# A two-block transformer kernel on one core: Fourier mixing folded along tokens, layer-norm tiles added before their sum over features, eight low halves formed by an accumulating DMA, rotary partners by shuffle

## The reference

```
def _fourier_mix(v, fw):
    vg = v.reshape(b, l, B_GROUPS, B_GROUP_DIM)            # 256 tokens, 4 groups of 128
    f = jnp.fft.fftn(vg, axes=(1, 3), norm='ortho').real
    return jnp.einsum('blgd,gde->blge', f, fw).reshape(b, l, B_WIDTH)

def _even_mix(h, ...):
    a_val, a_glu, a_gate, b_val, b_gate = _split(h @ w_in, ...)
    u = a_val * jax.nn.sigmoid(a_glu)
    u = jax.nn.silu(_layernorm(_dwconv(u, a_conv_w) + a_conv_b, a_ln_g, a_ln_b))
    y_a = (u @ a_pw_w + a_pw_b) * jax.nn.silu(a_gate)
    y_b = _fourier_mix(b_val, b_fw) * jax.nn.silu(b_gate)
    return jnp.concatenate([y_a, y_b], axis=-1) @ w_out
```

## Time and profile before

| | |
|---|---|
| median of 3 runs | 758.84 us (757.06 to 758.9) |
| the profiled execution | 758.82 us, of which the span is 756.7 us |
| PE busy / DVE busy / ACT busy | 98% / 86% / 51% of the span |
| POOL busy | 1.3 us, 10 instructions |
| granted TensorE clock, mean | 0.999 |
| HBM traffic | 154 MB read, 205 GB/s over the span |

### The profile page before, as it was taken

The page is one execution under the profiler, slowest core; times in us unless marked ns, Lnnn a source line. Parts: engine busy times, 40 slices in busy tenths (PEclk is TensorE's granted clock), DMA queues, the critical chain, the costliest instruction groups (busy, mean ns, idle before and its releaser), DMA issues.

```text
span 756.7 us, 12710 instructions
## 1 busy us (share of the span) xinstructions
PE 739.7 (98%) x5242; PEld 675.0 (89%) x5244; DVE 648.1 (86%) x1062; ACT 383.3 (51%) x530; POOL 1.3 (0%) x10
## 2 busy tenths in 40 slices
PE   8899999999999999999999999999999999999996
PEld 3689979999989999999999988888778899999995
DVE  5877799897998999999888999999989977788653
ACT  4264365668366554544566542222464345555642
POOL 0000000000000000000000000000000000000000
PEclk9999999999999999999999999999999999999999
DMA  9989999866555666666745252121106542575101
GB/s 365 418 320 402 376 386 348 317 246 239 176 215 213 234 223 244 256 231 252 252 159 174 101 225 99 70 98 69 56 0 247 215 141 91 177 278 215 56 2 55
DMA packets 23723, 155.92 MB, mean 206 GB/s; under 512 B 2630, under 2 KB 4463, under 8 KB 5232
## 3 DMA queue, kind: packets, MB, share of 16 engines
q1 hardware_dynamic: 21404, 150.37, 53.3%
q10 hardware_dynamic: 2262, 4.75, 2.0%
HBM read 154.04 MB, written 1.07 MB: 205 GB/s over the span
## 4 chain that ended last, share of the span: by engine, by line
PE 85%; DMA 6%; DVE 6%; ACT 2%; issue 1%; DVEq 0%; ACTq 0%; SPq 0%
PE psum L1529 70%; DMA raw<-in_w 4%; PE psum L1620 2%; DVE w_lo L896 2%; DMA arena<-in_w 2%; DVE w_lo L929 2%; ACT w_hi L400 1%; PE psum L1861 1%; PE psum L2034 1%; PE psum L2058 1%; PE psum L2046 1%; PE psum L1847 1%; PE psum L1711 1%; PE psum L1568 1%; PE psum L1693 1%
## 5 line engine op out<-in xcount | busy, mean ns | idle before, releaser
L1529 PE MATMUL psum<-h_hi,w_hi 128*128 128x256 f32 (+1 forms) x1280 | 386.9, 302 | 2.4 <-DVE w_lo L929 1.2
L1529 PE MATMUL psum<-h_lo,w_hi 128*128 128x256 f32 (+1 forms) x1280 | 382.5, 299 | 0.0
L1529 PE MATMUL psum<-h_hi,w_lo 128*128 128x256 f32 (+1 forms) x1280 | 382.5, 299 | 0.0
L1529 PEld LDWEIGHTS psum<-h_hi,w_hi 128*128 128x128 f32 x1280 | 244.5, 191 | 13.8 <-issue 2.6
L1529 PEld LDWEIGHTS psum<-h_lo,w_hi 128*128 128x128 f32 x1280 | 244.7, 191 | 8.0 <-issue 0.5
L1529 PEld LDWEIGHTS psum<-h_hi,w_lo 128*128 128x128 f32 x1280 | 244.6, 191 | 7.6
L929 DVE TENSOR_TENSOR w_lo<-raw,w_hi 128x2048 fp32r<-128x2048 f32 x90 | 205.9, 2288 | 28.7 <-ACT w_hi L400 27.7
L400 ACT CAST w_hi<-raw 128x2048 fp32r<-128x2048 f32 x90 | 171.2, 1905 | 38.5 <-DMA raw<-in_w 29.5
L896 DVE SCALAR_TENSOR_TENSOR w_lo<-raw,cond 128x1024 fp32r<-128x1024 f32 x88 | 104.2, 1220 | 0.8
L896 DVE SCALAR_TENSOR_TENSOR w_lo<-raw,arena 128x1024 fp32r<-128x1024 f32 x48 | 56.8, 1220 | 11.6 <-ACT arena L450 6.6
L621 ACT ACTIVATE arena<-psum,vec 128x256 f32<-128x256 f32 x44 | 22.5, 564 | 58.6 <-DVE g_lo L1171 54.2
(11 more groups left out here) (239 smaller groups left out, 707.4 us busy)
## 6 DMA issues: line engine op xcount, KB each, us to landing
raw<-in_w SPq DMA_DIRECT2D x138, 1024.0 KB, 5.0
arena<-in_w SPq DMA_DIRECT2D x3, 1024.0 KB, 13.9
xs<-in_xs SPq DMA_DIRECT2D x1, 1024.0 KB, 9.5
consts<-diff ACTq DMA_DIRECT2D x4, 256.0 KB, 10.1
cond<-diff ACTq DMA_DIRECT2D x1, 1024.0 KB, 8.7
xs<-in_xs ACTq DMA_DIRECT2D x1, 1024.0 KB, 7.4
out<-xs SPq DMA_DIRECT2D x2, 384.0 KB, 2.5
consts<-in_c ACTq DMA_DIRECT2D x1, 512.0 KB, 3.9
```

Of the source, the lines that this page charges most:

```text
L1529: last = mm(out, w[a], x[b], start=start and n == 0, stop=stop and n == 2, skip_group_check=skip)
```

## The change

1. Eight low halves (chunks `LIN_EIN`+4 to +11, `BY_DMA`): DVE no longer subtracts. ACT, after the cast, writes -`w_hi` into `w_lo` (a copy with scale -1), and a DMA issued by POOL adds `raw` onto it in SBUF, one such DMA at a time. Waits for `lo_done` become `remainder_ready`, which for these chunks waits for the DMA.
2. Fourier mixing: POOL folds the token axis about its middle (even and odd parts, three 128x508 operations for each pair of groups). The transform along features then makes 128 columns per matmul in place of 256, and that along tokens contracts over 128 in place of 256. The middle token comes in as a column (`fourier_middle`, four matmuls of 2 columns) that DVE adds when it gates. Groups 0 and 1 and the middle are moved ahead of PE's last projection chunk. ACT no longer copies the result out of PSUM; DVE gates straight from it, in four operations of 128x128 for each group in place of one of 128x512.
3. Layer norm: DVE adds the four tiles (and later their squares), so PE makes one sum by ones in place of four, twice.
4. `final_scaled`: four of eight tiles move behind the second `LIN_EOUT` chunk on DVE.
5. Rotary: partners by `stream_shuffle` on DVE in place of the swap matmuls; half of the queries' work moves ahead of `norm("odd_ctx", 7)`.
6. The constant tables get smaller (0.25 MB less to load).

The diff, cut to its core: removed lines stand in the functions printed above and are repeated only where the order of calls changes.

```diff
+BY_DMA = tuple(range(LIN_EIN + 4, LIN_EIN + 12))
+def remainder_of(j):
+    if j in BY_DMA:
+        return "lo_added", 16 * (BY_DMA.index(j) + 1)
+    return "lo_done", j + 1 - AS_LOADED - sum(i < j for i in BY_DMA)
...
+            def fold_tokens(pair):
+                pool.wait_ge(sem("ein_evac"), pair + 5)
+                v = b_val[:, 2 * pair:2 * pair + 2, :].rearrange("p g (s n) -> p (g s) n", s=2)
+                low, high = v[:, :, 1:P], v[:, :, P + 1:T][:, :, ::-1]
+                nc.gpsimd.tensor_tensor(high, low, high, ALU.subtract).then_inc(sem("differences"), 1)
+                pool.wait_ge(sem("differences"), 2 * pair + 1)
+                nc.gpsimd.tensor_tensor(low, low, low, ALU.add).then_inc(sem("differences"), 1)
+                pool.wait_ge(sem("differences"), 2 * pair + 2)
+                nc.gpsimd.tensor_tensor(low, low, high, ALU.subtract).then_inc(sem("folded"), 1)
+            for n, j in enumerate(BY_DMA):
+                if n in (3, 4):
+                    fold_tokens(n - 3)
+                pool.wait_ge(sem("negated"), n + 1)
+                if n:
+                    pool.wait_ge(sem("lo_added"), 16 * n)
+                pool.dma_start(w_lo[:, j % SPL, :].bitcast(F32), raw[:, RAW_OF_LIN[j] % RAW, :],
+                               accum_op=ALU.add).then_inc(sem("lo_added"), 16)
...
+                if i == 9:
+                    act.wait_ge(sem("fold_done"), 2)
+                    nc.scalar.activation(middle[:, 0:8], bank[1][:, 0:8], ACT.Copy, scale=DFT_SCALE).then_inc(sem("fold_ready"), 1)
+                    nc.scalar.activation(middle[:, 8:16], bank[1][:, 0:8], ACT.Copy, scale=-DFT_SCALE).then_inc(sem("fold_ready"), 1)
+                    fourier_evac(0)
+                    fourier_evac(1)
...
-            for g in range(2):
-                fourier_evac(g + 1)
-                fourier_out(g)
...
-            fourier_evac(3)
...
+                if t < 2:
+                    fourier_evac(t + 2)
+            act.wait_ge(sem("ln_sum"), 2)
+            me.mark(nc.scalar.activation(rstd[:, :], bank[3][:, :], ACT.Ln, bias=EPS_AP, scale=1.0 / 512))
...
+            def add_row(t):
+                dve.wait_ge(sem("conv_tap"), taps)
+                if t > 1:
+                    me.wait()
+                ins = nc.vector.tensor_tensor(row_sum, row_sum if t > 1 else conv[:, 0, :], conv[:, t, :], ALU.add)
+                if t < 3:
+                    me.mark(ins)
+                else:
+                    ins.then_inc(sem("rows_summed"), 1)
...
+            for t in range(1, 4):
+                dve.wait_ge(sem("ln_squares"), t + 1)
+                if t > 1:
+                    me.wait()
+                ins = nc.vector.tensor_tensor(row_sum, row_sum, ln_tmp[:, t, :], ALU.add)
+                if t < 3:
+                    me.mark(ins)
+                else:
+                    ins.then_inc(sem("rows_summed"), 1)
+            def fourier_gated(g):
+                dve.wait_ge(sem("four_b"), g + 1)
+                for s in range(2):
+                    for parity in range(2):
+                        out, src, gated = (by_parity(z, parity)[:, s] for z in (y_b[:, g, :], y_b_bank(g), sgate[:, 4 + g, :]))
+                        c = 8 * parity + 2 * g + s
+                        nc.vector.scalar_tensor_tensor(out, src, middle[:, c:c + 1], gated, ALU.add, ALU.mult
+                                                       ).then_inc(sem("y_b"), 1)
+            def final_scaled(ks):
+                for k in ks:
+                    nc.vector.scalar_tensor_tensor(xs[:, 0, k, :], xs[:, 0, k, :], col("g_final", k), rstd_x,
+                                                   ALU.mult, ALU.mult).then_inc(sem("final_scaled"), 1)
+            dve.wait_ge(sem("fold_ready"), 4)
+            fourier_gated(0)
...
-            for k in range(KT):
...
+            final_scaled(range(4))
...
-                if t in (2, 3):
-                    fourier_gated(t - 2)
+                if t == 1:
+                    fourier_gated(1)
...
-            dve.wait_ge(sem("final_scaled"), KT)
+            dve.wait_ge(sem("final_scaled"), 4)
             for i in range(4):
                 if i == 2:
+                    final_scaled(range(4, KT))
+                    dve.wait_ge(sem("final_scaled"), KT)
...
+            PARTNER = [i + 16 if i < 16 else i - 16 for i in range(32)]
+            def partners(half):
+                h = slice(512 * half, 512 * (half + 1))
+                dve.wait_ge(sem("q_raw"), half + 1)
+                me.mark(nc.vector.stream_shuffle(rot_tmp[:, h], q_raw[:, h], PARTNER))
+            def turn_queries(half):
+                me.wait()
+                for n in range(2):
+                    a = slice(512 * half + T * n, 512 * half + T * (n + 1))
+                    me.mark(nc.vector.tensor_tensor(rot_tmp[:, a], rot_tmp[:, a], rope_sin, ALU.mult))
+                    me.mark(nc.vector.tensor_tensor(q_raw[:, a], q_raw[:, a], rope_cos, ALU.mult))
+            dve.wait_ge(sem("c3_loaded"), 16)
+            partners(0)
+            turn_queries(0)
+            partners(1)
             norm("odd_ctx", 7)
...
+            turn_queries(1)
+            split(LIN_OIN + 3)
...
+            dve.wait_ge(sem("q_raw"), 3)
+            dve.wait_ge(sem("roped"), 1)
+            me.mark(nc.vector.stream_shuffle(rot_tmp[:, 0:T], k_raw, PARTNER))
+            me.wait()
...
+            me.mark(nc.vector.tensor_tensor(rot_tmp[:, 0:T], rot_tmp[:, 0:T], rope_sin, ALU.mult))
...
+                if g % 2 == 0:
+                    pe.wait_ge(sem("folded"), g // 2 + 1)
...
+                    pe.wait_ge(sem("four_ready"), g - 1)
...
+                    for part in range(2):
+                        c = slice(s * T + part * P, s * T + (part + 1) * P)
+                        last = mm(four_bank(g)[:, c], b_val[:, g, c], fold[:, g, part, :], start=True, stop=True)
+                last.then_inc(sem("four_a"), 1)
+            def fourier_b(g):
+                if g == 0:
+                    pe.wait_ge(sem("fold_ready"), 4)
+                elif g == 1:
...
+                pe.wait_ge(sem("four_ready"), g + 1 if g < 2 else 4)
+                for s in range(2):
+                    for part, table in enumerate((cos_l, sin_l)):
+                        c = s * T + part * P
+                        last = mm(y_b_bank(g)[:, s * T:(s + 1) * T], four[g][:, c:c + P], table, start=part == 0, stop=part == 1)
+                last.then_inc(sem("four_b"), 1)
...
+                if i == 9:
+                    fourier_middle()
+                    fourier_a(0)
+                    fourier_a(1)
...
-            fourier_a(0)
-            fourier_a(1)
+            pe.wait_ge(sem("rows_summed"), 1)
+            mm(bank[3][:, :], ones, row_sum, start=True, stop=True).then_inc(sem("ln_sum"), 1)
+            fourier_a(2)
+            fourier_a(3)
...
-            fourier_a(2)
...
-            for t in range(3):
-                ln_sum(t)
-            fourier_a(3)
-            ln_sum(3)
-            fourier_b(2, (0,))
...
-            fourier_b(2, (1,))
+            pe.wait_ge(sem("rows_summed"), 2)
+            mm(bank[3][:, :], ones, row_sum, start=True, stop=True).then_inc(sem("ln_sum"), 1)
+            fourier_b(2)
...
+            remainder_ready(LIN_PW)
...
-                    pe.wait_ge(sem("y_b_raw"), 4)
+                    pe.wait_ge(sem("y_b"), 8)
...
-            mm(bank[0][:, :], swap, q_raw[:, 0:512], start=True, stop=True)
-            mm(bank[1][:, :], swap, q_raw[:, 512:1024], start=True, stop=True).then_inc(sem("rot_done"), 1)
             keys_values(0, 1)
...
             keys_values(1, 1).then_inc(sem("lin_done"), 1)
...
-            mm(bank[2][:, 0:T], swap, k_raw, start=True, stop=True).then_inc(sem("rot_done"), 1)
```

More of the change, by code:

```diff
@@ L271, in halves, with four_bank @@
             return b[:, 0:T], b[:, T:2 * T]
-        def four_of(g, s):
-            return four[s + 2 if g == 3 else s]
-        def four_bank(g, s):
-            return wide[:, s, :] if g % 2 else bank[2 * s]
+        def four_bank(g):
+            return bank[2 if g % 2 else 0]
         def y_b_bank(g):
-            return wide[:, 2, :] if g % 2 else bank[1]
+            return (bank[1], wide[:, 2, :], bank[0], bank[2])[g]
+        row_sum = ln_tmp[:, 0, :]
+        middle = small[:, 8:24]
         def mod_row(base, v):
@@ L400, in split @@
                 nc.scalar.copy(w_hi[:, slot, :], raw[:, rslot, :]).then_inc(sem("hi_done"), 1)
+                if j in BY_DMA:
+                    nc.scalar.activation(w_lo[:, slot, :], raw[:, rslot, :], ACT.Copy, scale=-1.0).then_inc(sem("negated"), 1)
             def load_ln_exp():
@@ L694, in fourier_evac @@
             def fourier_evac(g):
[L695 to L705 removed]
+                act.wait_ge(sem("four_a"), g + 1)
+                nc.scalar.copy(four[g], four_bank(g)).then_inc(sem("four_ready"), 1)
             for i in range(10):
@@ L1304, in _ @@
```

(40 more changed lines are left out.)

105 lines of the change are left out of this document (33 added, 72 removed).

## The result

The changed kernel takes 746.59 us (median of four runs, 746.18 to 747.83) against 758.87 us before on the same chip: ratio 0.9846, 95% interval 0.9828 to 0.9864. On a second chip it took 746.49 against 757.73 us, ratio 0.985 (0.9836 to 0.9865). The prediction was 746.0 us. The profiled execution took 747.83 us, of which the span is 746.0.

What follows compares the result with a forecast made beforehand. PE, busy 98% of the span, was taken to bound the kernel. Terms 12.6 + 0.8 - 0.7 - 1.3 + 2.15 gave 13.5 us, less 0.7 for POOL: 12.8 off 758.82, so 746.0 us (forecast 744.5 to 748, range 743 to 755).

Steps and rivals of the forecast that it cites:

- PE's work: Matmuls, mainly Fourier mixing, sums by ones and rotary swaps: 16.9 us less on PE, after 0.8 added for narrow matmuls.
- DVE's end: End of DVE's convolution: from 541.2 to 524.4 us before any loss to POOL, leaving DVE 3.8 us to spare.
- The eight DMAs: Low halves in the even projection: 10 us per accumulating DMA, PE waiting for none while each stays under 12.3 us.
- The layer-norm chain: Last projection chunk to PE's restart: becomes the limit, restart at 541.15 instead of 553.75, gain 12.6 us.
- POOL against DVE: POOL's six fold operations beside DVE's taps: 5.2 us lost by DVE, between 0 and 7.2, costing 0.7 us.
- rival 2: POOL holds DVE up for whole operations or is slow itself: 750 us, up to 753; chance 0.18.
- taps above 0.48 us around the folds: Sign of being wrong: mean length of DVE's convolution taps above 0.48 us around POOL's folds.
- a wait of over 2 us for the row sum: Sign of being wrong: PE's `ones` matmuls waiting more than 2 us for DVE's row sum.
- `LIN_PW`: Pointwise projection: 0.8 us gained from two PE gaps, 0.7 lost waiting for the fourth low half of y.
- Squares: End of the even layer: moved half of `final_scaled` makes PE's sum of squares wait, 1.3 us lost (bounds 0 and 1.8).
- Odd layer: Rotary swap matmuls taken off PE, DVE's added work fitting its idle time: 2.15 us gained.
- What PE's microseconds are worth: Whole kernel: a microsecond of matmul removed is worth a microsecond until a chain through DVE or ACT is uncovered.

Runs made afterwards that it cites:

- dma_quarters: Changed kernel with each of the eight accumulating DMAs cut into four of 512 columns, one after the other; 781.36 us, ratio 1.0311.
- fold_dve: Changed kernel with the token folds moved from POOL to DVE, two operations per pair of groups instead of three; 745.01 us, ratio 0.9824.
- pe_filled: Changed kernel with nine bf16 matmuls of zeros on PE ahead of `LIN_PW`, where it idled 2.24 us; 745.61 us, ratio 0.9831.
- final_early: Changed kernel with item 4 undone: all eight `final_scaled` tiles stand behind the Fourier gates; 745.97 us, ratio 0.9838.
- final_gap: Changed kernel with four `final_scaled` tiles in DVE's wait for the first sum, the other four behind the gates; 746.88 us.
- sums_pe: Changed kernel with item 3 undone: PE sums rows and squares with eight matmuls, DVE has no adds; 747.52 us, ratio 0.9864.
- after_again: The changed kernel itself, run again unaltered as the measure on the second chip; 746.49 us.

## Why the prediction held, point by point

The two profiled executions differ by 10.7 us of span and 0.3 around it. By stretches: up to PE's restart 11.4 (553.75 in the earlier trace rows to 542.37; 0.5 of it is an earlier start: the last chunk but one already ends so much sooner), `LIN_PW` to the output projection -1.3 (14.04 before, 15.37 after), from there to the end of the squares -1.5, odd layer 2.05, end 0.1.

- **PE's work.** Right. Eight 128-column matmuls take 1.79 us, the four of 2 columns 0.81 (taken: 0.8, the upper end). The last chunk ends at 527.86, predicted 528.2.
- **DVE's end.** Right in sum: 524.4 + 5.2 = 529.6, measured 529.39.
- **The eight DMAs.** The forecast of 10 us was too slow, 7.2 measured; nothing hung on it, for the limit was put at 12.3 us. dma_quarters shows the mechanism behind that limit, not the limit itself. A weight load takes 4.9 us in the median in this kernel, so one accumulating DMA takes 1.5 times a load. The Trainium skill, Collectives: The Full Stack, "The bandwidth ceiling: the fold count and why AG ≠ RS ≠ AR", gives a factor of two for the ring's step that adds, from its two source reads. The 1.5 here, with issue and landing in both times, stays below that.
- **The layer-norm chain.** From the first sum's start to Ln I had 7.3 us. Measured: 7.26, but with DVE late. fold_dve, where it isn't, shows 7.9 (527.36 to 535.27), and there PE waits 0.49 us for the last add. The undersized terms are the hand-overs: 1.16 us from the start of the second sum to Ln, for which I had 0.86, and 0.2 us ahead of ACT's evacuation of the chunk. From Ln to the restart: 5.64 predicted, 5.66 measured, idle 2.2 predicted, 2.24 measured.
- **POOL against DVE.** 5.2 us predicted, 5.4 measured, which is luck in part: POOL's six operations were put at 7.2 us and took 9.6, and the 5.2 was picked between 0 and 7.2. Of PE's 1.59 us of wait 0.9 goes through (7.26 + 1.59 - 7.9), 0.7 predicted. So rival 2 was wrong on the size. One sign that the prediction had named for being wrong did show, taps above 0.48 us around the folds (15.42/29 = 0.53); the other, a wait of over 2 us for the row sum, didn't (1.59). What the prediction missed is that the same folds cost DVE less than half when it does them itself. The longest tap beside them is 1.51 us, near a tap of 0.47 plus one fold of 1.1. The Trainium skill, SBUF — State Buffer, "Who interferes with whom", says that a DVE instruction with two inputs in SBUF contends with a GpSimd instruction that reads SBUF. The trace agrees in kind, while the loss is 5.4 of the 9.6 us, not all.
- **`LIN_PW`.** This step failed. I gave it +0.8 for two gaps and -0.7 for the stall behind it, 0.1 us of gain, and left PE's clock out. The gaps went, the stall came out at 0.56 us (1.0 predicted), and without a fall the stretch takes 13.8 us (541.59 to 555.37 in pe_filled), 0.3 less than before. But the clock fell: -1.6 us, so 1.3 us were lost. I had worked out both idle times of PE (0.35 and 2.2) and drew nothing from them.
- **Squares.** -1.3 predicted, -1.5 measured; final_early and final_gap show the cause. Its counterpart was left out: final_early gains only 0.6 and not 1.5, since 0.9 us comes back at the restart.
- **Odd layer.** 2.15 predicted, 2.05 measured.
- **What PE's microseconds are worth.** The sum rests on "a microsecond of matmul removed is worth a microsecond until a chain is uncovered". sums_pe shows how far past that point the change goes: without the 5.2 us of item 3 removed, the restart is only 1.7 us later, so 3.5 of them bought idle time, and with that idle time came the fall of the clock.

Against the sum of 12.8 us the trace gives 11.0, of which 0.5 is the earlier start: 2.3 us are missing. `LIN_PW` is 1.4 short (+0.1 forecast, -1.3 measured), which the clock's 1.6 more than explains; the stretch up to the restart 1.0 (11.9 forecast with POOL's cost, 10.9 measured), squares and odd layer 0.3; 0.4 came back at the end and outside the span. The medians give 12.3 and 11.2. That the median lies only 0.6 us above the forecast is in part luck: the profiled execution, for which the same 746.0 was forecast, took 747.83, and the 1.3 us between the traces of after and after_again arise in the first block, which the forecast says nothing about.

## What to carry to other kernels

Before taking work off a saturated engine, ask which engine's work it covered, and move that first: here one half of the change loses 1.3%, the other does nothing, and both together gain 1.5%. Count the idle times that a shorter chain leaves on PE, since they can cost clock behind them, and put something into them (worth 1.6 us in the trace here). An operation given to POOL beside a DVE that streams from SBUF is not free; if DVE can do it in less than POOL would hold it up, leave it there.

## What the runs showed of the hardware

- PE's clock fell to 1.2 GHz for 3.4 us after idle times of 1.59 and 2.24 us with 10.7 us of matmuls between them. It didn't fall in the traces with 1.62 and 0.30 (pe_filled), 0.49 and 2.24 (fold_dve), 0.51 (sums_pe). It fell again with 1.62 and 2.24 (final_gap) and with 1.59 and 3.15 (final_early), for about as long. Such idle times don't settle it alone: near 22 us PE waits 1.33 to 2.04 us for weights in all thirteen traces, and the clock falls there in eight of them (after a wait of 2.04 in after_again) and not in five (2.00 in before, 1.98 in fold_dve). What tells them apart isn't shown. The Trainium skill, TensorE: Matmul & The Clock Gate, "What's actually happening", says that the clock is set by how busy PE has been recently; the traces of `LIN_PW` agree, those near 22 us don't tell.
- An accumulating DMA of 1 MB within SBUF takes 7.2 us in the median from POOL's issue (7.0 to 7.5 in the other runs), one of 256 KB 3.3 us (up to 7.4), and the issue holds POOL 0.86 to 1.00 us in either case. They ran beside weight loads of 1 MB that took 4.9 us in the median (5.0 before).
- A stream shuffle of 128x512 f32 takes DVE 0.73 to 0.75 us, priced at 0.6; of 128x256, 0.45 us.
